# First two modulation vectors by blocks of 128 columns, with the first two weight units of a norm multiplied side by side

## The reference, cut to what matters

```python
def ada_params(cond, w, b):                       # w: 1024 x 9*1024 for each layer
    m = (jax.nn.silu(cond) @ w + b)[..., None, :]
    return jnp.split(m, N_MOD, axis=-1)           # nine vectors of 1024
def modulate(x, shift, scale):
    return x * (1 + scale) + shift
def ffn_half(x, mods, g, w_gu, w_d):
    shift, scale, gate = mods
    h = modulate(rmsnorm(x, g), shift, scale) @ w_gu
    hg, hu = jnp.split(h, 2, axis=-1)
    return x + 0.5 * gate * ((jax.nn.silu(hg) * hu) @ w_d)
```

## Time and profile before

| what | value |
|---|---|
| three runs | 1949.94 us median, 1946.14 to 1950.98 |
| profiled execution, its own time | 1950.95 us |
| its span | 1949.2 us |
| mean granted TensorE clock | 0.971 of full |
| TensorE matmul busy | 1844.9 us (95%) |
| VectorE, ScalarE, GpSimd busy | 887.5, 614.6, 36.3 us |
| HBM read | 250.15 MB, 129 GB/s over the span |
| f0's first matmul, its third unit | 48.52 us, 76.55 us from the start of the span |

### The profile page before, as it was taken

How to read it: one execution, slowest core, us unless ns; L and a number is a source line. 1 busy time by engine, 2 the same in 40 slices (tenths; PEclk the granted TensorE clock), 3 DMA queues, 4 the chain that set the end, 5 groups by cost and what they waited for, 6 DMA issues and landing times.

```text
span 1949.2 us, 25181 instructions
## 1 busy us (share of the span) xinstructions
PE 1844.9 (95%) x10094; PEld 1491.5 (77%) x10094; DVE 887.5 (46%) x1375; ACT 614.6 (32%) x824; POOL 36.3 (2%) x72
## 2 busy tenths in 40 slices
PE   3999999999889999999999999999998998899996
PEld 1788778868544668888888688888877988589996
DVE  2433323345878552333334533333344455865555
ACT  2322122233445332212222322222223133244342
POOL 0000000000001000000000000000000000000000
PEclk7999999999899989999999999999998999999998
DMA  8522452243148353222213422232232224045553
GB/s 337 218 86 87 173 194 86 75 164 124 44 163 306 137 193 131 82 96 103 106 64 111 169 90 92 81 108 108 68 126 111 87 88 151 1 176 186 179 178 103
DMA packets 39108, 252.39 MB, mean 129 GB/s; under 512 B 4465, under 2 KB 5873, under 8 KB 14449
## 3 DMA queue, kind: packets, MB, share of 16 engines
q1 hardware_dynamic: 29232, 179.91, 26.3%
q0 software_dynamic: 9792, 71.31, 9.5%
HBM read 250.15 MB, written 1.05 MB: 129 GB/s over the span
## 4 chain that ended last, share of the span: by engine, by line
PE 87%; DVE 7%; ACT 2%; DMA 2%; issue 2%; SPq 0%; ACTq 0%; DVEq 0%
PE ps L396 26%; PE ps L398 26%; PE ps L397 26%; PE ps L432 3%; PE ps L596 1%; DMA xT<-in_xT 1%; DVE w_lo L1083 1%; DVE y L1266 1%; PE ps L570 1%; PE ps L743 1%; ACT w_hi L805 1%; PE ps L456 1%; PE ps L579 1%; DVE t_ring L1144 1%; PE ps L710 0%
## 5 line engine op out<-in xcount | busy, mean ns | idle before, releaser
L396 PE MATMUL ps<-hn_hi,w_hi 128*128 128x512 f32 (+2 forms) x1784 | 646.3, 362 | 12.4 <-DVE hn_lo L1160 8.2
L397 PE MATMUL ps<-hn_lo,w_hi 128*128 128x512 f32 (+2 forms) x1784 | 640.4, 359 | 0.0
L398 PE MATMUL ps<-hn_hi,w_lo 128*128 128x512 f32 (+2 forms) x1784 | 640.1, 359 | 0.0
L1083 DVE TENSOR_TENSOR w_lo<-raw,w_hi 128x2048 fp32r<-128x2048 f32 (+2 forms) x184 | 377.0, 2049 | 569.7 <-ACT w_hi L805 569.6
L805 ACT ACTIVATE w_hi<-raw 128x2048 fp32r<-128x2048 f32 (+2 forms) x184 | 316.6, 1721 | 823.5 <-PE ps L398 814.2
L396 PEld LDWEIGHTS ps<-hn_hi,w_hi 128*128 128x128 f32 (+1 forms) x1784 | 338.8, 190 | 77.3 <-issue 24.4
L398 PEld LDWEIGHTS ps<-hn_hi,w_lo 128*128 128x128 f32 (+1 forms) x1784 | 338.9, 190 | 50.5 <-issue 0.3
L397 PEld LDWEIGHTS ps<-hn_lo,w_hi 128*128 128x128 f32 (+1 forms) x1784 | 339.1, 190 | 48.4 <-issue 0.7
L396 PE MATMUL ps<-a_hi,w_hi 128*128 128x512 f32 (+1 forms) x704 | 258.9, 368 | 1.8 <-DVE a_lo L1198 1.8
L398 PE MATMUL ps<-a_hi,w_lo 128*128 128x512 f32 (+1 forms) x704 | 258.5, 367 | 0.0
L397 PE MATMUL ps<-a_lo,w_hi 128*128 128x512 f32 (+1 forms) x704 | 258.5, 367 | 0.0
(11 more groups left out here) (181 smaller groups left out, 1182.6 us busy)
## 6 DMA issues: line engine op xcount, KB each, us to landing
raw<-in_w_up SPq DMA_DIRECT2D x88, 1024.0 KB, 4.9
mod_raw<-in_mod_w POOLq DMA_DIRECT2D x68, 1024.0 KB, 7.1
raw<-in_w_downA SPq DMA_DIRECT2D x32, 768.0 KB, 4.3
raw<-in_w_downB SPq DMA_DIRECT2D x32, 640.0 KB, 3.9
raw<-in_w_od_in SPq DMA_DIRECT2D x16, 1024.0 KB, 4.8
raw<-in_w_ev_in SPq DMA_DIRECT2D x7, 1024.0 KB, 4.9
mod_raw<-in_mod_w SPq DMA_DIRECT2D x4, 1024.0 KB, 11.0
raw<-in_w_ev_out SPq DMA_DIRECT2D x4, 1024.0 KB, 4.9
```

The lines of the kernel that those rows point to most:

```text
L396: pe.matmul(o, lh, rh, start=first, stop=False)
L397: pe.matmul(o, lh, rl, start=False, stop=False)
L398: return pe.matmul(o, ll, rh, start=False, stop=last)
L1083: dve.tensor_tensor(w_lo[:, u0 % 2, 0:n], raw[:, u0 % 2, 0:n], w_hi[:, u0 % 2, 0:n], ALU.subtract).then_inc(lo_made, 1)
```

## The change

- SP loads x in four quarters right behind c, each with its own semaphore, then sel, mats, cols. Squares start with the first quarter; Silu of c comes after them on ScalarE.
- Weights of vectors 0 and 1 lie on the host as `mod_first`: eight blocks of 1 MB, block b with the 128 columns b of both vectors. All are loaded by SP, into the four places of `mod_raw` in turn: block 0, unit 0, block 1, unit 1, blocks 2 to 7; from block 4 on SP waits for the products of block b-4. GpSimd's queue starts with job 2.
- For each block b: products (16 instructions), row, columns (4 instructions), bias and gain on VectorE, then block k = b of the norm. On TensorE the products and columns of block k+1 stand ahead of the wait for block k of the norm; on ScalarE row k stands ahead of `hn_hi` k, and `head(1)` behind `hn_hi` 0; on VectorE `rest(1)` stands behind `hn_lo` 0.
- Behind norms 0, 1, 2, 3 and 5 the first two units go side by side: for k = 0 to 4 both units' six matmuls, then k = 5 to 7 of the first, what rode between the two units, and k = 5 to 7 of the second. Behind norm 4 nothing changes.
- `sel` gets two columns more and is padded to 32.
- Counts of `mod_row`, `mod_tr` and `mod_made` shift by six (`vector_done`).

```diff
             sp.dma_start(c_in, t["c_in"]).then_inc(par_in, 16)
-            sp.dma_start(sel[:], t["sel"]).then_inc(par_in, 16)
+            for i in range(4):
+                sp.dma_start(xT[:, 2 * i:2 * i + 2], t["xT"][:, 2 * i:2 * i + 2]).then_inc(x_in[i], 16)
+            sp.dma_start(sel[:, 0:10], t["sel"]).then_inc(par_in, 16)
             sp.dma_start(mats[:], t["mats"]).then_inc(par_in, 16)
             sp.dma_start(cols[:], t["cols"]).then_inc(par_in, 16)
-            for q in range(4):
-                sp.dma_start(mod_raw[:, 2 * q:2 * q + 2], t["mod_w"][0][:, 2 * q:2 * q + 2]).then_inc(mod_first[q], 16)
-            sp.dma_start(xT[:], t["xT"]).then_inc(x_in, 16)
+
+            def block(b):
+                if b >= 4:
+                    sp.wait_ge(mod_mm, b - 3)
+                sp.dma_start(block_place(b), t["mod_first"][b]).then_inc(mod_first[b % 4], 16)
+
+            block(0)
             load(U["f0upA"], 0, 0, t["w_up"][0, 0], UNIT)
+            block(1)
+            load(U["f0upA"], 1, 0, t["w_up"][0, 1], UNIT)
+            for b in range(2, KT):
+                block(b)
...
+            def block_products(b):
+
+                pe.wait_ge(mod_first[b % 4], 16 * (b // 4 + 1))
+                if b > 0:
+                    pe.wait_ge(mod_row, b)
+                for i in range(2):
+                    for g in range(4):
+                        last = pe.matmul(ps[32 * g:32 * g + 32, 4, 0:LAT], c_act[:, 2 * g + i, :],
+                                         block_place(b)[:, 2 * g + i, :], start=(i == 0), stop=(i == 1))
+                last.then_inc(mod_mm, 1)
+
+            def block_columns(b):
+                pe.wait_ge(mod_row, b + 1)
+                if b > 0:
+                    pe.wait_ge(mod_made, b)
+                for m in range(2):
+                    last = pe.matmul(ps[:, 5, 2 * m:2 * m + 2], mrow[:, m * P:(m + 1) * P], sel[:, 8:10],
                                      start=True, stop=True)
                 last.then_inc(mod_tr, 1)
...
             def hn_ready(n):
                 def ready(k):
+                    if n == 0 and k + 1 < KT:
+                        block_products(k + 1)
+                        block_columns(k + 1)
                     pe.wait_ge(hn_made, KT * n + k + 1)
...
+            SIDE = 5
+
+            def first_units(u0, n, w, between=None):
+
+                ready = hn_ready(n)
+                order = [(j, k) for k in range(SIDE) for j in range(2)]
+                order += [(j, k) for j in range(2) for k in range(SIDE, KT)]
+                for j, k in order:
+                    if j == 0:
+                        ready(k)
+                    if k == 0:
+                        begin(u0 + j)
+                    for b in range(2):
+                        o = b * KT * P + k * P
+                        last = three(ps[:, bank(u0 + j, b), 0:w], weights(u0 + j, o, o + P),
+                                     (hn_hi[:, k, 0:w], hn_lo[:, k, 0:w]), k == 0, k == KT - 1)
+                    if k == KT - 1:
+                        last.then_inc(unit_mm, 1)
+                        if j == 0 and between:
+                            between()
...
-            mod_products(0, 0, 4)
-            mod_columns(0)
             norm(0)
-            mod_products(1, 0, 4)
-            mod_columns(1)
+            block_products(0)
+            block_columns(0)
             ffn("f0", 0, 0, TOK)
             norm(1)
...
-            act.wait_ge(par_in, 64)
-            act.activation(c_act[:].rearrange("p k c -> p (k c)"), c_in, ACT.Silu).then_inc(c_made, 1)
-            act.wait_ge(x_in, 16)
             for d in range(KT):
+                act.wait_ge(x_in[d // 2], 16)
                 if d >= 2:
                     act.wait_ge(sq_added, d - 1)
                 act.activation(sq[:, d % 2, :], xT[:, d, :], ACT.Square).then_inc(sq_made, 1)
-            mod_rows(0)
+            act.wait_ge(par_in, 64)
+            act.activation(c_act[:].rearrange("p k c -> p (k c)"), c_in, ACT.Silu).then_inc(c_made, 1)
             norm_root(0)
             head_of(0)
-            mod_rows(1)
-            norm_heads(0)
-            head_of(1)
+            for k in range(KT):
+                act.wait_ge(mod_mm, k + 1)
+                if k > 0:
+                    act.wait_ge(mod_tr, k)
+                act.activation(mrow, ps[:, 4, 0:LAT], ACT.Copy).then_inc(mod_row, 1)
+                norm_head(0, k)
+                if k == 0:
+                    head_of(1)
...
+            dve.wait_ge(par_in, 64)
             norm_rstd(0)
             rest_of(0)
-            mod_vector(1)
-            norm_gain(0)
-            norm_apply(0)
-            rest_of(1)
+            dve.wait_ge(rstd_mm, 1)
+            for k in range(KT):
+                block_vectors(k)
+                norm_scaled(0, k)
+                norm_rest(0, k)
+                if k == 0:
+                    rest_of(1)
```

More of the change, by code:

```diff
@@ L163, in build @@
         a_made = sem("a_made")
-        x_in = sem("x_in")
+        x_in = [sem(f"x_in{i}") for i in range(4)]
         sq_made = sem("sq_made")
@@ L341, in ffn @@
                 for part, n in zip("AB", PARTS):
[L342 to L346, removed]
+                    first = 1 if name == "f0" and part == "A" else 0
                     with sp.Fori(first, n // 2) as r:
@@ L381, in _ @@
         def _(pool):
-            for m in range(1, JOBS):
+            for m in range(2, JOBS):
                 if m == JOBS - 1:
@@ L436, in mod_columns @@
             def mod_columns(m):
[L437 to L439 removed]
+                pe.wait_ge(mod_row, vector_done(m))
+                pe.wait_ge(mod_made, vector_done(m - 1))
                 for b in range(2):
[L441 removed]
+                    last = pe.matmul(ps[:, column_bank(m), 8 * b:8 * b + 8], mrow[:, b * P:(b + 1) * P], sel[:, 0:8],
+                                     start=True, stop=True)
+                last.then_inc(mod_tr, 1)
+            def block_products(b):
[13 more added lines that the diff above has]
+                    last = pe.matmul(ps[:, 5, 2 * m:2 * m + 2], mrow[:, m * P:(m + 1) * P], sel[:, 8:10],
                                      start=True, stop=True)
@@ L475, in pair @@
                         first = isinstance(r, int) and r == 0
+                        if first and part == "A":
+                            first_units(up, n, w, (lambda: mod_products(up_job, 0, 4)) if up_job else None)
+                            if up_job:
+                                mod_columns(up_job)
+                            return
                         for j in range(2):
-                            unit(up + j, r, 2, KT, w, (hn_hi, hn_lo), lambda b, k: b * KT * P + k * P,
-                                 hn_ready(n) if first and j == 0 and part == "A" else None)
+                            unit(up + j, r, 2, KT, w, (hn_hi, hn_lo), lambda b, k: b * KT * P + k * P)
                             if first and up_job and j == 0:
@@ L516, in two @@
                 return b * KT * P + k * P
-            for c in range(2):
-                unit(E + c, 0, 2, KT, TOK, (hn_hi, hn_lo), two, hn_ready(1) if c == 0 else None)
+            first_units(E, 1, TOK)
             def rotate(i):
@@ L816, in norm_root, with norm_head @@
                     .then_inc(sd_made, 1)
+            def norm_head(n, k):
+                act.wait_ge(t_made, KT * n + k + 1)
+                for s in streams(W[n]):
+                    last = act.activation(hn_hi[:, k, tokens(s)], t_ring[:, k % 2, tokens(s)], ACT.Identity,
+                                          bias=modT[:, 3 * n, k, s:s + 1])
+                last.then_inc(hn_hi_made, 1)
             def norm_heads(n):
-                w = W[n]
                 for k in range(KT):
[L821 to L825, removed]
+                    norm_head(n, k)
                     if k == 2 and n in NORM_JOB:
@@ L1151, in norm_apply @@
                             dve.wait_ge(y_out[k % 2], 16 * (k // 2))
-                        scaled(k)
+                        norm_scaled(n, k)
                     return
-                scaled(0)
+                norm_scaled(n, 0)
                 for k in range(KT):
                     if k + 1 < KT:
[L1157 to L1163, removed]
+                        norm_scaled(n, k + 1)
+                    norm_rest(n, k)
                 if n in NORM_JOB:
```

70 lines of the change are left out of this document (42 added, 28 removed).

## The result

The changed kernel takes 1936.89 us (median of five runs, 1935.41 to 1938.67), the kernel before 1950.77 (five runs, 1946.14 to 1951.27). The profiled execution took 1935.41 us, of it 1933.6 span, against 1950.95 and 1949.2 before; it is the fastest of the changed kernel's five.

What follows compares the result with a forecast made beforehand. TensorE, busy 95% of the span, was taken to bound the kernel. The start's 5.8 us less 3.3 lost at the other norms took 2.5 off 1950.95; with the median 1.0 lower, 1947.4 us, range 1941 to 1954.

Steps and rivals of the forecast that it cites:

- The start: From x's load to job 2's columns: earlier x and block-wise weights bring those columns to 70.4 from 76.19, gaining 5.8 us.
- the extra table load: On ScalarE at the start, Silu of c behind the squares costs a table load of 1.28 us (between 0 and 1.28).
- The cycle: Blocks 1 to 4 of both units at the start: TensorE's order sets a period of 4.65 us.
- Block 7's wait: At the start, unit 0 alone: TensorE idles 2 us ahead of block 7, then 2 us added for half clock.
- Norm 3: Pairing behind this norm gains 1.7 us and loses 0.9 to the evacuation wait: 0.8 us gained.
- Norm 1: Pairing behind this norm, at half clock with no idle time to give: 0 gained, 0.9 us lost.
- Norm 2: Pairing behind this norm, at half clock, with job 13 covering the wait: 0, at most 0.3 us gained.
- Norm 5: Pairing behind this norm loses 2.5 us to the evacuation wait and 0.7 to possible half clock after it.
- B: Rival: the clock falls in the start's block cycle; half the work at 0.50 costs 17 us, 1964; chance 0.08.
- A: Rival: no extra table load, full clock through block 0 and after block 7, 0.7 saved at norm 5: 1941.4; chance 0.17.
- C: Rival: the evacuation wait does not bind and pairing gives norm 3's 1.7 us in full: 1942.4; chance 0.07.
- D: Rival: blocks or x land late, or the cycle is a us longer; the start gives nothing: 1953; chance 0.06.

Runs made afterwards that it cites:

- q1_hn32: Kernel before with sel padded to 32 and only hn_hi and hn_lo moved 32 bytes past a multiple of 128: 1961.57 us against 1949.19, ratio 1.006.

## Why the prediction was wrong

**The step that failed** is "The padding and the shifted counts I cost at nothing; no row shows either, bounds 1 us each way." The padding alone measured 12.2 us. The same by rows: 1584 matmuls of 512 columns read `a` (528 a group, three groups), a down unit's 36 shortened by 8.446 - 8.172 = 0.27 us, 7.6 ns each: 12.0 us. The bound was no bound, since nothing stood behind it but that no instruction is added. A sign was to be had before: the earlier trace rows give 1.36/6 = 0.227 us for a matmul of an up unit; a down unit's 36 matmuls in 8.44 us are 0.2346. Same shape, same clock, no waits, and I did not ask why 36 took 0.27 us more than 36 x 0.227. With 12.2 off, the forecast would have been 1935.2, 1.7 from the measured time.

**The start** was right in mechanism, and in size 6.05 us for 5.8 in this execution, 3.4 and 4.5 in the two others with its code. x's quarter came at 4.85 for 5, the extra table load was there with its 1.28 us, ending at 12.29. The first matmul was 1.7 us early: the granted clock was 1.00 from 12 to 22 us where the forecast had half, so block 0's columns ended at 20.7 instead of 21.5, its products running in 1.54 us and not 1.94, and from block 1's columns to the matmul it was 0.46 us (25.18 to 25.64) where 1.1 stood for half clock. Three other executions with the blocks had that matmul at 26.97 to 27.66 (forecast 27.3). The cycle was too short by 0.33 us, in small terms all over it: from the first unit matmul to the next products 2.94 us (37.19 to 40.12) for 2.72, the last of the twelve alone 0.32 (39.80 to 40.12), from products to columns 1.58 (35.14 to 36.72) for 1.53, from columns on 0.47 (36.72 to 37.19) for 0.4; over four cycles it takes 1.3 us of this back. Block 7's wait was 1.78 (2 forecast), and the clock fell behind it: job 2's products took 4.66 us for 3.66.

**The norms.** Norm 3 gave 0.5 for 0.8. Norm 1 lost 1.5 for 0.9. Norm 2 gave 2.1 where at most 0.3 stood: the forecast took half clock there for granted, and at the full clock pairing has idle time to remove. Norm 5 lost 3.9 for 3.2: the forecast wait of 2.5 us is there, and behind it the granted clock was 0.50 (the last window above), the first matmul taking 0.58 us instead of 0.28; what the wait doesn't explain, 1.4, stands where 0.7 was put for that clock. The waits ahead of the third units behind norms 1, 3 and 5 of the changed kernel:

```profile
452.84 0.68 DVE L1325 TENSOR_TENSOR upad<-gact,ps 128x512 f32<-128x512 f32 x1
...
453.67 0.47 PE L411 MATMUL ps<-hn_hi,w_hi 128*128 128x512 f32 x1 [1.07 <-DVE upad L1325]
...
1095.76 0.50 PE L411 MATMUL ps<-hn_hi,w_hi 128*128 128x512 f32 x1 [0.85 <-DVE prod L1266]
...
1735.68 0.41 DVE L1266 TENSOR_TENSOR prod<-gact,ps 128x256 f32<-128x256 f32 x1
...
1736.14 0.58 PE L411 MATMUL ps<-hn_hi,w_hi 128*128 128x256 f32 x1 [2.50 <-DVE prod L1266]
```

Two products and 2.50 us of idle time: the evacuation of unit 0 stands behind `rest` of the third unit, as argued, and three blocks don't cover it.

**The rivals.** B fell: from 31.80 to 59.00 us the granted clock was 1.00, TensorE busy 23.05 of 27.2 us. The Trainium skill (TensorE: Matmul & The Clock Gate, "A second HAM failure mode: psum-queue depth-cycling") lets the clock swing where short idle times come between groups; this trace does not agree for the gap of 0.50 us ahead of each block's columns. It does show half clock behind block 7's idle 1.78 us: 1.00 up to 59.65 us, 0.60 on to 61.30, 0.50 on to 63. A and C, 1941.4 and 1942.4, lie nearest to the measured time, and for reasons that were mostly not there: the table load, the half clock behind block 7's and norm 5's waits and the waits for the evacuation all came. Of A only the full clock of block 0's products was there. D did not happen.

The Trainium skill's other figure (ScalarE: Activation LUTs, "Table sets: the hidden batching unit"), 2.7 us for a switch, was not borne out at 11.00 us: the last Square ended at 10.98, the load took 1.28, and the next function ran at 12.29.

## What to carry to other kernels

## What the runs showed of the hardware

- Matmuls in fp32r of 128 rows, 512 columns, full clock: 0.227 us each where moving and stationary operand start equally far past a multiple of 128 bytes, 0.234 where they differ by 32, 64 or 96: 3% of the pace of an engine that is busy 95% of the time. (10.889/48 and 8.172/36, against 8.446, 8.412 and 8.412/36.)
- With 256 columns (f3) the sign is reversed for the up units: 5.769/48 = 0.1202 us where they start equally, 5.609/48 = 0.1169 where the moving operand is 32 bytes further on (5.64 a unit in `q1_hn32`, at the same distance), 5.69 a unit where the stationary one is 32 further on. For the down units it isn't so simple: 4.21 to 4.27 with `a` 32, 64 or 96 further on, but 4.33 both at equal starts and with `w` 32 further on. This is also why the changed kernel's f3 lost 0.9 us: its down units of 12 blocks went from 4.23 to 4.33 as `a` came to a multiple of 128. Why is open: no run varied anything but the starts.
- The Trainium skill (SBUF — State Buffer, "Operand start alignment") has a rule for where an operand may start, its element size, and says of it: "This is about legality, not speed". All kernels here keep it, and starts alone move them from 0.9937 (padding) to 1.0102 (`w` off) of the kernel before.
